# An encoder layer on one core: up- and down-projection as two phases with activations through DRAM, the up-projection with seven block products

## The chip, the core and the metric

The kernel runs on one core of one Trainium2 chip. The metric is the device time of one execution in microseconds. The kernel before took 1589.59 us, the median of three runs (1588.44 to 1590.68).

## The reference

One layer for 1536 tokens (a prompt of 512 and a sample of 1024) of width 1024: attention and a pooling mixer, an output projection into the residual, and then a feed-forward part, which the change is about.

```python
x = x + jnp.concatenate([a, p], axis=-1) @ w_out
h2 = rmsnorm(x, norm2_g)
x = x + jnp.square(jax.nn.relu(h2 @ w_up)) @ w_down    # hidden width 4096
```

All in float32. On the chip each float32 product is made of three matmuls on operands split in a high and a low part (`w_hi m_hi + w_hi m_lo + w_lo m_hi`), which the helper `three` issues.

## The kernel before

The program gives each engine its own list of instructions, in an order written out by hand; engines wait for each other by semaphores (`wait_ge`), and each engine works its list strictly from first to last. All DMAs are issued by SyncE and share one queue.

The **output projection** runs over 12 tiles of 128 tokens. TensorE makes `project_out(t)`, 48 matmuls of 512 columns, and then transposes the tile before (`transpose_x2`). VectorE adds the residual, ScalarE squares and sums (`square_x2`), GpSimd takes the power (`norm_x2`), VectorE scales (`scale_x2`), and after the transposes ScalarE copies the high part of h2 and VectorE subtracts the low part (`split_h2`). `split_c` makes the two parts of the next tile's input. h2 for all tokens stays in SBUF, high and low.

The **feed-forward part** runs over 16 chunks of 2 x 128 hidden channels (`mlp_chunk`) and in each over 3 blocks of 512 tokens. The up-projection is an ordinary product (`up_block`, 8 slices of the input width, `three` for each, 512 tokens wide). The down-projection uses the Strassen-Winograd scheme: the 2 x 2 block product (hidden channels by tokens and output columns) takes seven block products (`down_product`) instead of eight, of sums of blocks. `sum_hid` makes the sums of the hidden activations on VectorE, `sum_wd` those of the weights on GpSimd. Each product has its two PSUM banks, and VectorE adds it into one or more quarters of `yacc` in SBUF (`accumulate`). The two projections are interleaved: after each of the first products follow two slices of the next block's up-projection, after each later one three.

The names that matter: `three` lines 562 to 566, `project_out` 746 to 766, `transpose_x2` 769 to 775, ScalarE's and VectorE's parts of the feed-forward part from lines 1100 and 1434, `accumulate` line 1471, `sum_wd` lines 1712 to 1728, SyncE's loads lines 495 to 552. ScalarE's copies are all recorded at line 848, VectorE's low parts at line 1190.

## Time and profile before

| | |
|---|---|
| median of the runs | 1589.59 us |
| the profiled execution's own time | 1589.55 us |
| its span | 1587.7 us |
| TensorE busy | 1551.5 us, 98% |
| VectorE busy | 1079.1 us, 68% |
| ScalarE busy | 637.6 us, 40% |
| GpSimd busy | 386.9 us, 24% |
| mean granted TensorE clock | 0.996 |
| DMA, mean over the span | 52 GB/s |

The profile shows one execution. Busy shares tell how full an engine is, not whether it sets the end; the chain of waits, followed back from the last instruction, tells that. The records of two matmuls in a row overlap, so the time that one costs is the distance between two starts, not its record.

### The profile page before, as it was taken

The numbers are of one execution on the slowest core, as the hardware profiler recorded it, in microseconds if no ns is written. First come the engines' busy times: TensorE is split into PE (matmuls) and PEld (weight loads), VectorE is DVE, ScalarE is ACT, GpSimd is POOL, SyncE is SP. The second block draws the span as 40 slices with busy tenths as digits, with TensorE's granted clock in tenths as the row PEclk, the third lists the DMA queues.
The fourth block names the chain that finished last, engine by engine and source line by source line (L and its number), as shares of the span: only waits on it lengthen the run. The fifth ranks groups of instructions, "written<-read, shape, count | busy, mean of one in ns | idle before, by whom it ended". The sixth has DMA issues, their size and how long they took to land.

```text
span 1587.7 us, 21963 instructions
## 1 busy us (share of the span) xinstructions
PE 1551.5 (98%) x7616; PEld 1296.3 (82%) x7616; DVE 1079.1 (68%) x1285; ACT 637.6 (40%) x1016; POOL 386.9 (24%) x369
## 2 busy tenths in 40 slices
PE   6999989999999999999999999999999999999998
PEld 5999867888778888888888888888888888888886
DVE  6534479999964446767667667667667667677676
ACT  5223269999962223323323323333233233233231
POOL 3423677888850001101101101001001001011010
PEclk9999999999999999999999999999999999999999
DMA  6110021000122225011011011001101100110103
GB/s 226 47 44 17 17 81 34 12 13 13 51 99 94 81 91 225 27 41 40 26 40 40 26 40 34 32 26 40 40 26 40 40 26 26 43 37 26 40 27 146
DMA packets 28230, 82.19 MB, mean 52 GB/s; under 512 B 3105, under 2 KB 5281, under 8 KB 28193
## 3 DMA queue, kind: packets, MB, share of 16 engines
q1 hardware_dynamic: 28192, 81.70, 15.1%
q8 instruction: 22, 0.36, 0.1%
q14 instruction: 16, 0.12, 0.0%
HBM read 64.39 MB, written 12.58 MB: 48 GB/s over the span
## 4 chain that ended last, share of the span: by engine, by line
PE 70%; DVE 1%; issue 0%; DVEq 0%
PE ps L564 21%; PE ps L566 20%; PE ps L565 20%; PE ps L760 6%; PE ps L766 3%; PE ps L775 1%; DVE yacc L1471 0%; DVE hidlo L1190 0%; DVE hraw L1453 0%; DVEq L1450 0%
## 5 line engine op out<-in xcount | busy, mean ns | idle before, releaser
L1471 DVE TENSOR_TENSOR yacc<-yacc,ps 128x1024 f32<-128x1024 f32 x336 | 410.1, 1221 | 274.4 <-PE ps L566 273.1
L564 PE MATMUL ps<-h2hi,wuhi 128*128 128x512 f32 x768 | 298.9, 389 | 0.0
L566 PE MATMUL ps<-h2hi,wulo 128*128 128x512 f32 x768 | 298.8, 389 | 0.0
L565 PE MATMUL ps<-h2lo,wuhi 128*128 128x512 f32 x768 | 298.8, 389 | 0.0
L564 PE MATMUL ps<-wdhi,hidhi 128*128 128x512 f32 x672 | 262.0, 390 | 2.2 <-DVE hidlo L1190 1.7
L566 PE MATMUL ps<-wdhi,hidlo 128*128 128x512 f32 x672 | 261.5, 389 | 0.0
L565 PE MATMUL ps<-wdlo,hidhi 128*128 128x512 f32 x672 | 261.4, 389 | 0.0
L1717 POOL TENSOR_TENSOR wdraw<-wdraw,wdraw 128x512 f32<-128x512 f32 x16 | 20.8, 1298 | 738.9 <-DMA wdraw<-in_w_down 738.9
L1106 ACT ACTIVATE hraw<-ps 128x512 f32<-128x512 f32 x96 | 57.2, 596 | 314.6 <-PE ps L566 314.6
L848 ACT ACTIVATE hidhi<-hraw 128x768 fp32r<-128x768 f32 x96 | 91.4, 952 | 215.4 <-PE ps L566 215.1
L566 PEld LDWEIGHTS ps<-h2hi,wulo 128*128 128x128 f32 x768 | 144.1, 188 | 30.0
L565 PEld LDWEIGHTS ps<-h2lo,wuhi 128*128 128x128 f32 x768 | 144.2, 188 | 29.9
L564 PEld LDWEIGHTS ps<-h2hi,wuhi 128*128 128x128 f32 x768 | 144.1, 188 | 29.8
L564 PEld LDWEIGHTS ps<-wdhi,hidhi 128*128 128x128 f32 x672 | 126.1, 188 | 30.2 <-DVE hidlo L1190 2.2
L566 PEld LDWEIGHTS ps<-wdhi,hidlo 128*128 128x128 f32 x672 | 126.1, 188 | 26.3
L565 PEld LDWEIGHTS ps<-wdlo,hidhi 128*128 128x128 f32 x672 | 126.1, 188 | 26.1
L1190 DVE TENSOR_TENSOR pTlo<-ps,pThi 128x512 fp32r<-128x512 f32 x160 | 107.7, 687 | 22.8 <-ACT pThi L848 21.3
L1190 DVE TENSOR_TENSOR hidlo<-hraw,hidhi 128x768 fp32r<-128x768 f32 x96 | 110.3, 1149 | 5.8 <-ACT hidhi L848 5.8
L662 PEld LDWEIGHTS ps<-ident,prob 128*128 128x128 f32 x640 | 78.9, 141 | 33.0 <-issue 6.3
L1628 POOL TENSOR_SCALAR prob<-prob,rinv 128x1024 f32<-128x1024 f32 (+1 forms) x96 | 95.5, 1003 | 39.5 <-DVE rinv L1252 38.3
L662 PE MATMUL ps<-ident,prob 128*128 128x128 f32 x640 | 97.6, 275 | 7.0 <-POOL prob L1628 5.6
L848 ACT ACTIVATE pThi<-ps 128x512 fp32r<-128x512 f32 x160 | 95.4, 601 | 18.8 <-PE ps L662 13.9
(124 smaller groups left out, 2549.8 us busy)
## 6 DMA issues: line engine op xcount, KB each, us to landing
wuraw<-in_w_up SPq DMA_DIRECT2D x32, 512.0 KB, 3.3
wdraw<-in_w_down SPq DMA_DIRECT2D x32, 512.0 KB, 3.3
xin<-in_x SPq DMA_DIRECT2D x12, 512.0 KB, 3.4
x2in<-in_x SPq DMA_DIRECT2D x12, 512.0 KB, 3.5
out_y<-x2in SPq DMA_DIRECT2D x12, 512.0 KB, 2.9
yacc<-out_y SPq DMA_DIRECT2D x3, 2048.0 KB, 13.7
out_y<-yacc SPq DMA_DIRECT2D x12, 512.0 KB, 2.8
woraw<-in_w_out SPq DMA_DIRECT2D x2, 2048.0 KB, 7.5
```

The source lines that it names most:

```text
L564: pe.matmul(out, w_hi, m_hi, start=start, stop=False, skip_group_check=resumed)
L565: pe.matmul(out, w_hi, m_lo, start=False, stop=False, skip_group_check=resumed)
L566: return pe.matmul(out, w_lo, m_hi, start=False, stop=stop, skip_group_check=resumed)
L662: mm = pe.transpose(ps[:, 4 + k % 3, qt * P:(qt + 1) * P], prob[s.parity(pair, idx)][:, u, c0:c0 + P], ident[:])
L760: pe.matmul(ps[:, 2 * i + h], c[:, i, k], wohi[:, k, h * 512:(h + 1) * 512], start=(k == 0 and c is chi), stop=False)
L766: mm = pe.matmul(ps[:, 2 * i + h], chi[:, i, k], wolo[:, k, h * 512:(h + 1) * 512], start=False, stop=(k == KT - 1))
L848: return act.activation(out, in_, ACT.Copy, **kw)
L1106: act.activation(out, ps[:, 6 + f].rearrange("p (a c) -> p a c", a=2), ACT.Relu).then_inc(relu_done, 1)
L1190: return dve.tensor_tensor(out, a, b.bitcast(F32), ALU.subtract)
L1471: dve.tensor_tensor(q, q, gather_banks(b, o), ALU.add).then_inc(acc_done, 1)
L1628: ins = pool.tensor_scalar(p, p, rinv[:, b, q:q + 1], 1.0, ALU.mult, ALU.mult)
L1717: pool.tensor_tensor(b12, b22, b12, ALU.subtract).then_inc(wd_sum, 1)
```

## The change

The feed-forward part becomes two phases. In the **up phase** 32 steps make the hidden activations, each for one chunk of 256 hidden channels and one of two groups of 768 tokens, in which the tokens stand as two halves of 3 x 128 = 384. The product is a 2 x 2 scheme too (channels and input width, and tokens), with seven products of four slices, 384 columns each. The sums of h2 blocks are made once, while the output projection runs (`lo_h2`); for group 0 the 14 arrays (11.0 MB) go to a DRAM tensor `h2d` and come back before step 2, those of group 1 stay. The sums of w_up are made on VectorE (`sum_wu`), the products are gathered in PSUM with copies and sums (`save_u` on ScalarE, `sum_u` on VectorE), then come relu and square, then the block sums of the hidden activations (`sum_hid`), and seven blocks (1.4 MB) of each step go to DRAM (`store_hid`) from buffers `hout` that exist once.

In the **down phase** 8 chunks of 512 hidden channels by 3 units of 512 tokens take 7 products each; a product now runs over two hidden slices in PSUM, 12 matmuls, before it is accumulated, so there are 168 accumulations and not 336. The hidden blocks are loaded in three parts per unit (`load_hid`), split by `hi_part` and `lo_part`, and the weights of the next chunk are split meanwhile (`hi_wd`, `lo_wd`) into the other of two sets of buffers.

The core of the diff, SyncE first (its order of stores and loads):

```diff
+            def load_wu(w, c):
+                if not (isinstance(w, int) and w == 0):
+                    sp.wait_ge(wu_lo, SLOTS * w)
+                sp.dma_start(wuraw[:], w_up[bass.ds(2 * c, 2)].rearrange("f p k n -> p f k n")).then_inc(wu_in, 16)
...
+            for p in range(TT):
+                if p == TT - 1:
+                    sp.wait_ge(c_hi, TT)
+                    sp.wait_ge(c_lo, TT)
+                    load_wu(0, 0)
+                store_x2(p)
+                if p in (3, 5, 7):
+                    store_h2((p - 3) // 2)
+                if p + 2 < TT:
+                    load_x2(p + 2)
+            def store_hid(n, c, g):
+                for i, (ready, count) in enumerate(((raw_done, 4 * n + 3), (hid_sum, 4 * n + 3), (hid_sum, 4 * n + 4))):
+                    sp.wait_ge(ready, count)
+                    sp.dma_start(hd[i][bass.ds(c, 1), :, 3 * (1 - g):3 * (1 - g) + 3].rearrange("a p q s c -> (a p) q s c"),
+                                 hout[i][:]).then_inc(h_out[i], 16)
+            load_wu(1, 1)
+            sp.wait_ge(out_done, TT)
+            sp.wait_ge(xT2_done, TT)
+            for o in range(SLOTS):
+                for q in range(QT_TILES):
+                    sp.wait_ge(h2_stored[q], 16 if q == 1 else 32)
+                sp.dma_start(h2[0][o][:].rearrange("p a q k c -> p a (q k c)").bitcast(F32),
+                             h2d[2 * o:2 * o + 2].rearrange("a p q c -> p a (q c)")).then_inc(h2_in[o], 16)
...
+            store_hid(0, 0, 1)
+            load_wu(2, 2)
+            store_hid(1, 1, 1)
```

TensorE, with what each product waits for:

```diff
+            def up_product(s, w, g, par, o):
+                pe.wait_ge(wu_lo, SLOTS * w + o + 1)
+                if isinstance(s, int) and s == 0:
+                    pe.wait_ge(h2_lo, SLOTS * 5 + 2 if o < 2 else SLOTS * 6)
+                if isinstance(s, int) and s == 2:
+                    pe.wait_ge(h2_in[o], 16)
+                if not (isinstance(s, int) and s < 2):
+                    if o == 0:
+                        pe.wait_ge(relu_done, 4 * s - 4)
+                    if o == 1:
+                        pe.wait_ge(u_sum, 3 * s - 5)
+                    if o == 3:
+                        pe.wait_ge(u_sum, 3 * s - 3)
                 if o == 2:
+                    pe.wait_ge(u_copied, 3 * s + 1)
+                if o == 4:
+                    pe.wait_ge(u_copied, 3 * s + 2)
+                if o == 5:
+                    pe.wait_ge(u_copied, 3 * s + 3)
+                if o == 6:
+                    pe.wait_ge(u_sum, 3 * s + 2)
+                for k in range(4):
+                    mm = three(up_bank(par, o), wuhi[o][:, k], wulo[o][:, k], h2[g][o][:, 0, :, k], h2[g][o][:, 1, :, k],
+                               o in OPENS and k == 0, k == 3, o not in OPENS)
+                mm.then_inc(up_done, 1)
+            def up_step(s, w, g, par):
+                for o in range(SLOTS):
+                    up_product(s, w, g, par, o)
...
+            def down_product(n, z, u, o):
+                m = UNITS * n + u
+                if u == 0:
+                    pe.wait_ge(wd_lo, SLOTS * n + o + 1)
+                if o in (0, 2, 5):
+                    pe.wait_ge(hid_lo, 3 * m + part_of(o)[0] + 1)
+                if isinstance(m, int) and m == 0 and o in (1, 3):
+                    pe.wait_ge(relu_done, 8 * CHUNKS)
+                    pe.wait_ge(u_sum, 6 * CHUNKS)
                 pe.wait_ge(acc_done, SLOTS * m + (2, 6, SLOTS + 1, SLOTS, SLOTS + 3, SLOTS + 4, SLOTS + 5)[o])
-                banks = gather_banks(b, o)
-                for j in range(2):
...
+                banks = down_banks(u, o)
+                i, j = part_of(o)
+                for q in range(2):
+                    for k in range(2):
+                        mm = three(banks[:, q], hidhi[i][:, k, q, j], hidlo[i][:, k, q, j],
+                                   wdhi[z][o][:, k], wdlo[z][o][:, k], o in OPENS and k == 0, k == 1, o not in OPENS)
                 mm.then_inc(down_done, 1)
...
+            for p in range(1, TT):
+                project_out(p)
+                transpose_x2(p - 1)
+            up_product(0, 0, 1, 0, 0)
+            up_product(0, 0, 1, 0, 1)
             transpose_x2(TT - 1)
```

ScalarE, relu and square of a step, and its order in the down phase:

```diff
+            def square_relu(s, par, k):
+                if k < 3:
+                    act.wait_ge(u_sum, 3 * s + k + 1)
+                    src = (u1, u1, u2)[k][:].rearrange("p (q c) -> p q c", q=QT_TILES)
+                else:
+                    act.wait_ge(up_done, SLOTS * s + SLOTS)
+                    src = up_bank(par, 6)
+                out = h12[:] if k == 3 else out_slot((0, 5, 1)[k])
+                if not (isinstance(s, int) and s == 0):
+                    act.wait_ge(hid_sum, 4 * s)
+                    if k < 3:
+                        act.wait_ge(h_out[(0, 2, 0)[k]], 16 * s)
+                act.activation(out, src, ACT.Relu).then_inc(relu_done, 1)
+                act.wait_ge(relu_done, 4 * s + k + 1)
+                act.activation(out, out, ACT.Square).then_inc(raw_done, 1)
...
+            def down_chunk(n, z, last=False):
+                for u in range(UNITS):
+                    m = UNITS * n + u
+                    for i in range(3):
+                        if not (last and u == UNITS - 1):
+                            hi_part(m + 1, i)
+                        if not last:
+                            for o in (((), (0, 1), ()), ((2,), (3,), ()), ((4,), (5,), (6,)))[u][i]:
+                                hi_wd(n + 1, 1 - z, o)
             act.wait_ge(z_act, GROUPS)
```

VectorE, the last tiles of the output projection, the sums of an odd tile of h2, the order of a step, and that of a chunk of the down phase:

```diff
+            for p in range(1, TT):
+                if p + 1 < TT:
+                    split_c(p + 1)
+                else:
+                    for o in range(2):
+                        lo_wu(0, o)
+                    for k in range(4):
+                        sum_wu(0, k)
+                    for o in range(2, SLOTS - 1):
+                        lo_wu(0, o)
+                residual(p)
+                if p % 2 == 0:
+                    scale_x2(p)
+                    lo_h2(p - 1)
+                else:
+                    lo_h2(p - 1)
+                    scale_x2(p)
+            lo_h2(TT - 1)
+            lo_wu(0, SLOTS - 1)
...
+                raw = {o: h2_full(q, o) for o in (2, 3, 4, 5)}
+                dve.wait_ge(xT2_done, p + 1)
+                dve.wait_ge(h2_b11, q + 1)
+                dve.tensor_tensor(raw[4], h2_bank(q, 2), raw[5], ALU.subtract).then_inc(h2_sum, 1)
+                dve.wait_ge(h2_hi, SLOTS * q + 3)
+                dve.wait_ge(h2_sum, 4 * q + 1)
+                dve.tensor_tensor(raw[2], h2_bank(q, 3), raw[4], ALU.subtract).then_inc(h2_sum, 1)
+                dve.wait_ge(h2_sum, 4 * q + 2)
+                dve.tensor_tensor(raw[3], raw[2], raw[5], ALU.subtract).then_inc(h2_sum, 1)
+                dve.wait_ge(h2_sum, 4 * q + 3)
+                dve.tensor_tensor(raw[5], h2_bank(q, 1), raw[2], ALU.subtract).then_inc(h2_sum, 1)
+                minus(h2_half(q, 6, 1), h2_bank(q, 3), h2_half(q, 6, 0)).then_inc(h2_lo, 1)
+                dve.wait_ge(h2_sum, 4 * q + 4)
+                for n, o in enumerate((4, 2, 3, 5)):
+                    dve.wait_ge(h2_hi, SLOTS * q + 4 + n)
+                    minus(h2_half(q, o, 1), raw[o], h2_half(q, o, 0)).then_inc(h2_lo, 1)
...
+            def up_step(s, par, prep=None, late=None, sums=True, first_down=False):
+                if sums:
+                    for k in range(4):
+                        sum_hid(s - 1, k)
+                if late is not None:
+                    lo_wu(late, 6)
+                if first_down:
+                    lo_wd(0, 0, 0)
+                if prep is not None:
+                    lo_wu(prep, 0)
+                sum_u(s, par, 0)
+                if prep is not None:
+                    lo_wu(prep, 1)
+                if first_down:
+                    lo_wd(0, 0, 1)
+                    lo_wd(0, 0, 2)
+                    lo_part(0, 0)
+                sum_u(s, par, 1)
+                if prep is not None:
+                    sum_wu(prep, 0)
+                    sum_wu(prep, 1)
+                if first_down:
+                    lo_wd(0, 0, 3)
+                sum_u(s, par, 2)
+                if prep is not None:
+                    sum_wu(prep, 2)
+                    sum_wu(prep, 3)
+                    for o in range(2, 6):
+                        lo_wu(prep, o)
+                if first_down:
+                    for o in range(4, SLOTS):
+                        lo_wd(0, 0, o)
+            def lo_wd(n, z, o):
+                dve.wait_ge(wd_hi, SLOTS * n + o + 1)
                 if o == 2:
-                    dve.wait_ge(wd_sum, 4 * c + 4)
...
+            def down_chunk(n, z, last=False):
+                for u in range(UNITS):
+                    m = UNITS * n + u
+                    more = not (last and u == UNITS - 1)
+                    def lo_wds(*slots):
+                        for o in slots:
+                            if not last:
+                                lo_wd(n + 1, 1 - z, o)
+                    accumulate(n, u, 0)
+                    accumulate(n, u, 1)
+                    if more:
+                        lo_part(m + 1, 0)
+                    accumulate(n, u, 2)
+                    lo_wds(*((), (2,), (4,))[u])
+                    accumulate(n, u, 3)
+                    lo_wds(*((0,), (), ())[u])
+                    accumulate(n, u, 4)
+                    if more:
+                        lo_part(m + 1, 1)
+                    accumulate(n, u, 5)
+                    lo_wds(*((1,), (3,), (5,))[u])
+                    accumulate(n, u, 6)
+                    if more:
+                        lo_part(m + 1, 2)
+                    lo_wds(*((), (), (6,))[u])
+            up_step(0, 0, prep=1, sums=False)
...
+            up_step(2 * CHUNKS - 1, 1, late=CHUNKS, first_down=True)
+            lo_part(0, 1)
+            for k in range(4):
+                sum_hid(2 * CHUNKS - 1, k)
+            lo_part(0, 2)
+            down_chunk(0, 0)
```

## Rows read from the trace of the kernel before

**Rows 1.** The page, busy time by engine: busy us, share, instructions.
```profile
PE 1551.5 (98%) x7616; PEld 1296.3 (82%) x7616; DVE 1079.1 (68%) x1285; ACT 637.6 (40%) x1016; POOL 386.9 (24%) x369
```

**Rows 2.** The page, chain that ended last: by engine, by line.
```profile
PE 70%; DVE 1%; issue 0%; DVEq 0%
PE ps L564 21%; PE ps L566 20%; PE ps L565 20%; PE ps L760 6%; PE ps L766 3%; PE ps L775 1%; DVE yacc L1471 0%; DVE hidlo L1190 0%; DVE hraw L1453 0%; DVEq L1450 0%
```

**Rows 3.** Busy time by stretch, its length first, then engines, clock, DMA.
```profile
599.50:1567.50 968.00, 968.00 (x4277) 801.57 (x4276) 676.77 (x756) 304.45 (x432) 82.98 (x66) 1.00 0.13 43
```

**Rows 4.** Timeline, TensorE at its end: start us, us, instruction.
```profile
1582.78 0.40 PE L566 MATMUL ps<-wdhi,hidlo 128*128 128x512 f32 x1
```

**Rows 5.** The chain in order of time, output projection: start us, us.
```profile
457.46 8.77 PE ps L760 x32
469.86 7.25 PE ps L760 x32
583.20 3.63 PE ps L766 x16
598.64 0.87 PE ps L775 x8
```

**Rows 6.** Timeline of 256-column matmuls (first, last of 44); group of their loads.
```profile
74.20 0.28 PE L565 MATMUL ps<-hTlo,wihi 128*128 128x256 f32 x1
...
79.35 0.28 PE L566 MATMUL ps<-hThi,wilo 128*128 128x256 f32 x1
...
L565 PEld LDWEIGHTS ps<-hTlo,wihi 128*128 128x128 f32 x192 | 37.3, 194 | 0.2
```

**Rows 7.** Groups of instructions (busy us, mean ns); one stretch of three sums.
```profile
L1471 DVE TENSOR_TENSOR yacc<-yacc,ps 128x1024 f32<-128x1024 f32 x336 | 410.1, 1221 | 274.4 <-PE ps L566 273.1 <-issue 0.9
L1190 DVE TENSOR_TENSOR wdlo<-wdraw,wdhi 128x512 fp32r<-128x512 f32 x96 | 65.5, 684 | 0.0
L1453 DVE TENSOR_TENSOR hraw<-hraw 128x256 f32<-128x256 f32 x192 | 82.7, 431 | 6.1 <-ACT hraw L1108 1.9
L848 ACT ACTIVATE hidhi<-hraw 128x1024 fp32r<-128x1024 f32 x48 | 50.7, 1056 | 80.1 <-PE ps L566 79.9 <-DVE hraw L1453 0.2
L1728 POOL TENSOR_TENSOR wdraw<-wdraw,wd_t 128x512 f32<-128x512 f32 x16 | 20.8, 1302 | 0.0
1568.59 1.48 DVE L1453 TENSOR_TENSOR hraw<-hraw 128x256 f32<-128x256 f32 x3
```

**Rows 8.** Timeline of the steps after one tile's output projection.
```profile
492.71 1.22 DVE L1387 TENSOR_TENSOR x2in<-x2in,ps 128x1024 f32<-128x1024 f32 x1 [4.74 <-PE ps L766]
493.97 1.06 ACT L1066 ACTIVATE junk<-x2in 128x1024 f32<-128x1024 f32 x1 [8.75 <-DVE x2in L1387]
495.47 0.55 POOL L1538 TENSOR_TENSOR rsx<-msx,mexp 128x1 f32<-128x1 f32 x1
```

**Rows 9.** DMA: one stretch at full rate; issues, KB each, us to landing.
```profile
612.00:616.00 4.00, 4.00 (x20) 3.30 (x19) 3.12 (x5) 3.72 (x6) 1.43 (x2) 1.00 1.03 417
wuraw<-in_w_up SPq DMA_DIRECT2D x32, 512.0 KB, 3.3
rope<-in_rope SPq DMA_DIRECT2D x12, 64.0 KB, 1.9
pscale<-in_pool_scale SPq DMA_DIRECT2D x1, 2.0 KB, 8.8
```

**Rows 10.** TensorE after being idle, and the clock granted (before DMA share).
```profile
203.73 0.47 PE L644 MATMUL ps<-KA,Qs 128*128 128x512 f32 x1 [2.22 <-ACT prob L920]
205.00:208.00 3.00, 3.00 (x16) 2.90 (x16) 2.96 (x4) 1.38 (x4) 2.47 (x3) 0.57 0.00 0
456.25 0.50 PE L564 MATMUL ps<-dhi,wphi 128*128 128x512 f32 x1 [1.25 <-POOL dlo L1666]
1572.13 0.49 PE L564 MATMUL ps<-wdhi,hidhi 128*128 128x512 f32 x1 [1.73 <-DVE hidlo L1190]
```

More of the change, by code:

```diff
@@ L157, in hybrid_layer @@
+        hin = [at(f"hin{i}", hin_at[i], [2, 2, len(PARTS[i]), P]) for i in range(3)]
         ps = ctx.enter_context(nc.psum_tensor("ps", [P, 8, 512], F32))
@@ new lines, in load_ahead @@
+            def load_ahead(n, u, last=False):
+                if u == 0 and not last:
+                    load_wd(n + 1)
+                m = n, u + 2
+                if u:
+                    m = n + 1, u - 1
+                if not (last and u):
+                    for i in range(3):
+                        load_hid(*m, i)
+            with sp.Fori(0, DOWNS // 2 - 1) as h:
+                for z in range(2):
+                    for u in range(UNITS):
+                        load_ahead(h * 2 + z, u)
@@ new lines, in _ @@
+            up_step(0, 0, prep=1)
+            up_step(1, 1, late=1)
+            up_step(2, 0, prep=2)
+            with act.Fori(2, CHUNKS) as c:
+                up_step(2 * c - 1, 1, late=c)
+                up_step(2 * c, 0, prep=c + 1)
+            up_step(2 * CHUNKS - 1, 1, late=CHUNKS, first_down=True)
+            hi_part(0, 1)
+            hi_part(0, 2)
+            down_chunk(0, 0)
+            down_chunk(1, 1)
+            with act.Fori(1, DOWNS // 2 - 1) as h:
+                for z in range(2):
+                    down_chunk(h * 2 + z, z)
@@ L1736, in rope_tables @@
+            sum_wd(0, 0)
+            sum_wd(1, 1)
+            with pool.Fori(1, DOWNS // 2) as h:
+                for z in range(2):
+                    sum_wd(h * 2 + z, z)
 def rope_tables():
```

821 lines of the change are left out of this document (443 added, 378 removed).

## The prediction

> **What bounds the kernel now.** I read the page's busy row first: TensorE is busy 98% of the span, VectorE 68% [rows 1]. The chain of waits puts 70% of the span on TensorE and 61% on the three matmul lines of the helper `three`, in equal parts [rows 2]. The busy times by stretch then say where: from 599.5 to 1567.5 us, the feed-forward part, TensorE is never idle, in 4277 matmuls [rows 3]. Eight of these are transposes that take 0.87 us together [rows 5], so a matmul of 512 columns takes (968.0 - 0.87)/4269 = 0.2266 us. The last matmul starts at 1582.78 [rows 4]. All of the feed-forward part is 4320 such matmuls: 979 us, and with the transposes 979.8. It lasts 599.51 to 1583.0, so 3.7 us are lost, in the last unit. There is no slack on TensorE to win, so only fewer columns help, and every wait that the new order puts on TensorE costs its full length.
>
> The profiled execution took 1589.55 us for a span of 1587.7; the 1.85 us around it stay. It equals the median of the runs (1589.59).
>
> **Removed: one product in eight of the up-projection.** Before: 96 blocks (32 slices of the hidden width, 3 token blocks) of 8 x 3 matmuls of 512 columns, 2304. After: 32 steps of 7 products of 4 x 3 matmuls of 384 columns, 2688. No row has 384 columns. 256 columns take (79.35 - 74.20)/43 = 0.1198 us [rows 6]; the middle of that and 0.2266 is 0.1732. Ends: the rate per column of the 512 form gives 0.1700, that of the 256 form 0.1797. I take the middle, since both widths lie about 13 ns over columns/2.4 GHz. 2304 x 0.2266 - 2688 x 0.1732 = 522.1 - 465.6 = **-56.5 us** (ends -65.1 and -39.1). The new moving operand is read as three pieces of 128 columns; no row shows that, and I take it as free, as the ends hold a few per cent of it. The down-projection has 8 x 3 x 7 x 12 = 2016 matmuls, as before.
>
> The Trainium skill (TensorE: Matmul & The Clock Gate, "Back-to-back issue gap") gives N/2.4 + 2.5 ns for an isolated gap, 162.5 ns at 384 columns. By that the up-projection would take 436.8 us and be 29 us shorter still. But its value for 512 is 215.8, where this trace has 226.6, so I don't take it for the sum.
>
> **Removed: the 3.7 us at the end.** It came from a last unit that no up-projection covered. In the last unit now a product takes 12 x 0.2266 = 2.72 us and an accumulation 1.22 [rows 7], so nothing waits: **-3.7**. The 205 us of VectorE that half the accumulations save were beside TensorE: 0.
>
> **Added: work on h2 while the output projection runs.** A tile there takes 7.3 + 3.6 + 0.87 = 11.8 us of TensorE [rows 5]. VectorE's operations on 512 columns take 0.684, 0.61 apart, or 0.79 apart if each waits for the one before (at 256 columns one takes 0.43 and dependent ones stand 0.53 apart [rows 7]). For an odd tile it now has four dependent sums and five low parts, 6.1 us. They start when residual, ScalarE's square, GpSimd's power and the scaling are through, 4.7 us after the projection's end (residual to power, 492.71 to 495.47 + 0.55 [rows 8], then 1.2), and end at 10.8; the next transposes are due at 11.8. Hidden with 1.0 us to spare, the next `split_c` with 0.6: 0, at most 1 us on each of 5 tiles.
>
> **A. First up product.** Before, TensorE went straight on at 599.5. Now it needs tile 10's h2. At 597.6 VectorE is done with tile 9 (586.8 + 10.8), and then comes the new first weight chunk, ahead of `residual(11)`: 2 low parts, 4 dependent sums, 4 low parts, 1.2 + 3.2 + 2.4 = 6.8 us. So residual at 604.4, square to 606.8, two copies, two low parts: 608.8. **+9.3**.
>
> **B. The third product** needs all of tile 11: its transposes end at 613.9, then four sums, low part, four low parts, 6.3 us: 620.2. **+6.3**.
>
> **C, D. Behind the h2 reload.** SyncE issues the load of weight chunk 1 only when chunk 0's last low part is done (620.8), and it lands 4.7 later (3.3 for half its size, and half a megabyte more at full rate [rows 9]); ScalarE stands at it and TensorE's fifth product waits until 628.8: **+4.4**. Behind it in the same queue go 7 loads, 11.0 MB. At 410 GB/s [rows 9] the 12.1 MB end at 622.0 + 29.4 = 651.4. Only then comes `store_hid(0)`, for which `square_relu` of step 1 waits (`h_out`, the output buffer is single). One store more (1 us) and its completion (1.5) make 653.9; square_relu and `save_u(1)` follow, 1.5 us. The fifth product of step 1 starts at 655.5 and not at 643.4: **+12.1**. That transfers of one queue land in order is read from 2 KB that took 8.8 us behind others where 64 KB took 1.9 [rows 9]. Were they served side by side, D would be 0, and at 340 GB/s 18 us.
>
> **The 30 steps after that** take 12 x 7 x 0.1732 = 14.55 us each. I add 7.3 us on VectorE and 8 on ScalarE a step; the tightest place is `save_u(1)` of the odd steps, queued behind the weight sums and four low parts of the step before: it ends about 0.8 to 1.1 us before it is due. 0; it would be up to 1 us in 15 steps.
>
> **E. Up to down.** In step 31 VectorE's `lo_wd(0,0,2)` waits for GpSimd's third and fourth sum of 1024 columns (1.3 us for 512 [rows 7]; I take 2.2, with 2.6 as the end); `sum_u(1)` is queued behind it and the last up product waits for that: about 4 us. After the last product, square_relu, hi_part, lo_part, four sums and lo_part stand before `accumulate(0,0,0)`, for which the third down product waits. That is 9.4 us in all, **+9.4** (4 to 12).
>
> **F. One wait in each chunk of the down phase.** At the first unit of a chunk ScalarE runs `hi_part(m+1,1)` when product 4 ends, then `hi_wd(0)`; VectorE has `lo_wd(0)` queued before `accumulate 4`; product 6 waits for that accumulation. From the start of product 5: 0.16 + 0.1 (end of product 4 and hop), hi_part on 1536 columns 1.4, hi_wd 1.05, lo_wd 1.15, accumulation 1.22, hop 0.1 = 5.2 against 2.72 of cover. 2.5 us in 7 chunks: **+17.5** (0 to 21).
>
> **The clock.** After an idle of 1.25 us at 456.25 the granted clock fell to 1.2 GHz, and the 32 matmuls that take 7.25 took 8.77 [rows 5, 10]; after 2.22 us at 203.73 too (0.57 granted in 205 to 208); after 1.73 at 1572 not [rows 10]. So 1.5 us a fall: A, D and E surely (B and C's is inside D), F at about half: 6.5 x 1.5, **+9** (0 to 15).
>
> Sum: -56.5 - 3.7 + 9.3 + 6.3 + 4.4 + 12.1 + 9.4 + 17.5 + 9 = +7.8. Span 1595.5, time **1597**. That is slower by 0.5%.
>
> **Rivals.**
> 1. The wait of F is not there: VectorE isn't held by `lo_wd(0)`, since ScalarE's two copies come early enough. For it: VectorE has only 15 of 19 us a unit, and a chain under 2.72 us costs nothing. Against it: four rows in series already make 4.8. Then -17.5 and -5 of clock: 1575, faster. It decides at 2.72 us from product 4's end. Chance 0.27.
> 2. Columns cost less than I think: the 13 ns over columns/2.4 go away at 384 (2688 x 0.1600 = 430), -35 us: 1562, faster. Against it: two widths show the 13 ns. This is about what the skill's formula named above gives (its 162.5 ns, -29). Chance 0.04.
> 3. Weight loads bind: a load's record is 191 to 194 ns [rows 6], longer than a matmul of 384 columns now takes. If each had to end before the next began, 2688 x 0.191 = 513, +48: 1645. Against it: at 256 columns the same loads stand beside a pace of 120. Chance 0.03.
> 4. The steady steps are tighter than drawn (1 us in 15 steps, 1 in 5 tiles, 2 in E and D): +24: 1618. For it: margins under 1.1 us in three places. Chance 0.12.
> 5. The waits are a little shorter each, and the sum comes out level: 1589. Chance 0.1.
> My forecast: 0.44.
>
> **How the numbers follow.** A measurement of this kernel tells a change from none at about 0.2%, 3.2 us. Faster: rivals 1 and 2, 0.31. Same: rival 5 and a little of the forecast, 0.12. Slower: the rest of the forecast, rivals 3 and 4, 0.57. The range goes from rival 1 with 6 us below it, 1569, to rival 4, 1618; what is left out is rivals 2 and 3 and the tails. The likeliest case alone spans 1588 to 1610.
>
> **What would show it.** The 384-column matmuls start 0.173 us apart. TensorE is idle for some 9 us just after 599.5, 6 us before the third up product, then 4, then 12 where it is ScalarE's copy of u that releases it and ScalarE waits for a DMA of the output blocks. In the down phase TensorE is idle seven times for 2.5 us, released by an accumulation; between the steps of the up phase it is idle nowhere. I am wrong if the idle TensorE time after 599.5 is under 40 us in all, or if the pace is outside 0.170 to 0.180.

## The result and the profile after

The changed kernel took 1625.46 us (median of 4, 1617.37 to 1627.6), the kernel before 1589.13: a ratio of 1.0218, 95% interval [1.0182, 1.0254]. It is slower, as forecast, but by 36 us and not by 8, and above the range of the prediction (1569 to 1618). The profiled execution took 1625.35 us for a span of 1623.6, at a mean granted clock of 0.976.

The page after, busy time by engine (answers to [rows 1]) and the chain that ended last ([rows 2]):

```profile
PE 1520.8 (94%) x8000; PEld 1346.7 (83%) x8000; DVE 1041.2 (64%) x1290; ACT 731.3 (45%) x1231; POOL 386.7 (24%) x337
...
PE 77%; DVE 6%; issue 5%; POOL 5%; ACT 4%; DMA 3%; SPq 0%; DVEq 0%; ACTq 0%; POOLq 0%
```

TensorE is busy 31 us less and its share falls from 98 to 94%: it now waits. Where, the busy times by stretch say (columns as in [rows 3]; the clock, third from the end, is the granted share of 2.4 GHz, and the last two lines are single stretches at the lower level, 0.50 or 1.2 GHz, "half clock" below):

```profile
600.50:675.00 74.50, 44.45 (x223) 43.66 (x224) 30.16 (x49) 26.14 (x50) 0.74 (x2) 0.82 0.55 220
675.00:1090.00 415.00, 415.00 (x2397) 415.00 (x2396) 204.28 (x355) 212.34 (x412) 2.51 (x2) 1.00 0.36 135
1133.00:1618.00 485.00, 457.62 (x1943) 374.20 (x1942) 365.31 (x280) 127.22 (x116) 73.87 (x28) 0.96 0.37 120
605.50:612.00 6.50, 2.60 (x8) 2.63 (x9) 3.25 (x4) 2.71 (x5) 0.74 (x2) 0.50 0.20 81
1138.50:1144.50 6.00, 5.59 (x13) 4.51 (x14) 5.26 (x5) 0.09 (x1) 1.97 (x2) 0.50 0.30 85
```

The middle of the up phase is full: 2397 matmuls of 384 columns in 415 us, 0.1731 us each, at clock 1.00. The loss is in the first three steps (30 of 74.5 us idle, clock 0.82) and in the down phase (27 us idle, clock 0.96). Every wait of TensorE over 1 us after 600.5, from its timeline (start us, us, instruction, idle before and releaser; what was [rows 10] before), in the order of the prediction's terms, A, B, C, D, then E (four), then F (seven):

```profile
609.40 0.66 PE L729 MATMUL ps<-h,wuhi 128*128 128x384 f32 x1 [9.08 <-DVE h L1432]
622.08 0.66 PE L729 MATMUL ps<-h,wuhi 128*128 128x384 f32 x1 [6.08 <-DVE h L1432]
630.97 0.41 PE L729 MATMUL ps<-h,wuhi 128*128 128x384 f32 x1 [2.73 <-ACT u L1028]
658.13 0.66 PE L729 MATMUL ps<-h,wuhi 128*128 128x384 f32 x1 [12.33 <-ACT u L1028]
1095.37 0.41 PE L729 MATMUL ps<-h,wuhi 128*128 128x384 f32 x1 [1.92 <-ACT u L1028]
1101.64 0.41 PE L729 MATMUL ps<-h,wuhi 128*128 128x384 f32 x1 [1.87 <-ACT u L1028]
1109.99 0.41 PE L729 MATMUL ps<-h,wuhi 128*128 128x384 f32 x1 [3.95 <-DVE u L1735]
1122.44 0.47 PE L729 MATMUL ps<-wdhi,hidhi 128*128 128x512 f32 x1 [3.10 <-DVE yacc L1802]
1138.91 0.77 PE L729 MATMUL ps<-wdhi,hidhi 128*128 128x512 f32 x1 [5.31 <-DVE yacc L1802]
1202.08 0.50 PE L729 MATMUL ps<-wdhi,hidhi 128*128 128x512 f32 x1 [3.05 <-DVE yacc L1802]
1264.66 0.80 PE L729 MATMUL ps<-wdhi,hidhi 128*128 128x512 f32 x1 [3.56 <-DVE yacc L1802]
1325.78 0.80 PE L729 MATMUL ps<-wdhi,hidhi 128*128 128x512 f32 x1 [2.20 <-DVE yacc L1802]
1389.10 0.79 PE L729 MATMUL ps<-wdhi,hidhi 128*128 128x512 f32 x1 [4.33 <-DVE yacc L1802]
1453.64 0.80 PE L729 MATMUL ps<-wdhi,hidhi 128*128 128x512 f32 x1 [4.32 <-DVE yacc L1802]
1518.08 0.80 PE L729 MATMUL ps<-wdhi,hidhi 128*128 128x512 f32 x1 [4.20 <-DVE yacc L1802]
```

What D waits for shows on ScalarE, whose copy of `u` releases it: before that ScalarE waits for a store of the output blocks.

```profile
656.53 0.52 ACT L1311 ACTIVATE hout<-u 128x384 f32<-128x384 f32 x1 [16.04 <-DMA hd<-hout]
```

The starts of all matmuls give the account, term by term. For each one, the gap to the next start less the pace of its width is waiting, or clock where the granted clock is half and the gap only doubled. TensorE's part from the last transposes of the output projection to its end lasts 1018.8 us after (600.15 to 1618.99; before 599.51 to 1583.0, 983.5): 2688 x 0.1733 + 2016 x 0.2266 + 0.9 of transposes = 923.5, and 95.3 of losses.

| us lost in | predicted | measured |
|---|---|---|
| A, B, C, D, waiting | 32.1 | 30.9 |
| E, waiting | 9.4 | 11.5 |
| F, waiting | 17.5 | 28.8 |
| clock, all | 9 | 22.2 (5.7 beside A to D, 1.6 at E, 14.9 at F) |
| rest | 0 | 1.9 |

The waits here are up to 0.3 us longer each than in the rows, as a first matmul after a wait has a longer record. The down phase alone, F and its clock, lost 43.7 us.

What the seven waits of F are made of shows in three engines' timelines just before one of them (start us, us, instruction; at 1389.10 TensorE goes on):

```profile
1381.89 2.41 POOL L2044 TENSOR_TENSOR wdraw<-wdraw 128x1024 f32<-128x1024 f32 x1 [45.36 <-DMA wdraw<-in_w_down]
1384.48 2.35 POOL L2053 TENSOR_TENSOR wd_t<-wdraw 128x1024 f32<-128x1024 f32 x1 [0.18 <-POOL wdraw L2044]
...
1382.08 1.49 ACT L1028 ACTIVATE hidhi<-hin 128x1536 fp32r<-128x1536 f32 x1 [7.02 <-PE ps L731]
1383.48 1.98 ACT L1028 ACTIVATE wdhi<-wdraw 128x1024 fp32r<-128x1024 f32 x2
...
1384.55 3.36 DVE L1432 TENSOR_TENSOR wdlo<-wdraw,wdhi 128x1024 fp32r<-128x1024 f32 x1 [3.97 <-ACT wdhi L1028]
1387.83 1.21 DVE L1802 TENSOR_TENSOR yacc<-yacc,ps 128x1024 f32<-128x1024 f32 x1
```

The order is the one the prediction drew: `hi_part`, `hi_wd(0)`, `lo_wd(0)`, accumulate 4, product 6. But `lo_wd(0)` (the "split" of slot 0: VectorE subtracts the high part of a weight block from it) takes 3.36 us, where the prediction had 1.15. It is recorded from 1384.55, GpSimd's second sum from 1384.48 to 1386.83, and the split ends 1.08 us behind that sum, as if it had stood still until GpSimd was through. One chunk earlier the split began first, and there it is GpSimd that takes longer:

```profile
1323.36 1.23 DVE L1432 TENSOR_TENSOR wdlo<-wdraw,wdhi 128x1024 fp32r<-128x1024 f32 x1 [3.96 <-ACT wdhi L1028]
1323.42 3.39 POOL L2053 TENSOR_TENSOR wd_t<-wdraw 128x1024 f32<-128x1024 f32 x1 [0.18 <-POOL wdraw L2044]
```

The wait follows the split. In chunks 1 to 6 the splits of slot 0 take 2.07, 2.40, 1.23, 3.36, 3.34 and 3.23 us and the waits are 3.05, 3.56, 2.20, 4.33, 4.32 and 4.20: each time 0.97 to 1.16 us more than the split.

### The profile page after: what moved, and what is told of

Its sections match the earlier page's. It is cut to its first block, busy times and chain, and to the rows that moved or that the text cites. A ratio compares the mean times of both kernels' runs of the same rounds, so it can differ in the third digit from the quotient of the medians.

```text
span 1623.6 us, 23483 instructions
## 1 busy us (share of the span) xinstructions
PE 1520.8 (94%) x8000; PEld 1346.7 (83%) x8000; DVE 1041.2 (64%) x1290; ACT 731.3 (45%) x1231; POOL 386.7 (24%) x337
## 2 busy tenths in 40 slices
DMA packets 68789, 193.55 MB, mean 119 GB/s; under 512 B 5504, under 2 KB 7680, under 8 KB 68736
## 4 chain that ended last, share of the span: by engine, by line
PE 77%; DVE 6%; issue 5%; POOL 5%; ACT 4%; DMA 3%; SPq 0%; DVEq 0%; ACTq 0%; POOLq 0%
PE ps L729 20%; PE ps L730 20%; PE ps L731 20%; PE ps L925 5%; PE ps L827 3%; PE ps L931 2%; DMA wdraw<-in_w_down 1%; POOL prob L1954 1%; PE ps L842 1%; PE ps L843 1%; PE ps L809 1%; DMA hd<-hout 1%; PE ps L811 1%; DVE yacc L1802 1%; DVE nmax L1487 1%
## 5 line engine op out<-in xcount | busy, mean ns | idle before, releaser
L729 PE MATMUL ps<-h,wuhi 128*128 128x384 f32 x896 | 303.0, 338 | 38.0 <-ACT u L1028 18.9
L730 PE MATMUL ps<-h,wuhi 128*128 128x384 f32 x896 | 302.1, 337 | 0.0
L731 PE MATMUL ps<-h,wulo 128*128 128x384 f32 x896 | 301.9, 337 | 0.0
L1802 DVE TENSOR_TENSOR yacc<-yacc,ps 128x1024 f32<-128x1024 f32 x168 | 204.5, 1218 | 92.2 <-PE ps L731 91.8
L1028 ACT ACTIVATE hidhi<-hin 128x1024 fp32r<-128x1024 f32 (+1 forms) x72 | 86.6, 1205 | 352.5 <-PE ps L731 347.5
L2044 POOL TENSOR_TENSOR wdraw<-wdraw 128x1024 f32<-128x1024 f32 x8 | 19.1, 2391 | 790.2 <-DMA wdraw<-in_w_down 790.2
L729 PEld LDWEIGHTS ps<-h,wuhi 128*128 128x128 f32 x896 | 170.3, 190 | 39.8 <-issue 34.6
L1735 DVE TENSOR_TENSOR u<-u,ps 128x384 f32<-128x384 f32 x96 | 53.1, 553 | 198.9 <-PE ps L731 198.6
L730 PEld LDWEIGHTS ps<-h,wuhi 128*128 128x128 f32 x896 | 170.5, 190 | 0.0
L731 PEld LDWEIGHTS ps<-h,wulo 128*128 128x128 f32 x896 | 170.3, 190 | 0.0
L1432 DVE TENSOR_TENSOR hidlo<-hin,hidhi 128x1024 fp32r<-128x1024 f32 (+1 forms) x72 | 115.3, 1601 | 6.6 <-ACT hidhi L1028 6.6
L1311 ACT ACTIVATE hout<-u 128x384 f32<-128x384 f32 x96 | 50.4, 525 | 147.6 <-DVE u L1735 128.0
```

The costliest lines, as they stand in the source:

```text
L729: pe.matmul(out, w_hi, m_hi, start=start, stop=False, skip_group_check=resumed)
L730: pe.matmul(out, w_hi, m_lo, start=False, stop=False, skip_group_check=resumed)
L731: return pe.matmul(out, w_lo, m_hi, start=False, stop=stop, skip_group_check=resumed)
L1028: return act.activation(out, in_, ACT.Copy, **kw)
L1311: act.activation(out, src, ACT.Relu).then_inc(relu_done, 1)
L1432: return dve.tensor_tensor(out, a, b.bitcast(F32), ALU.subtract)
```

## The experiments

The theory after the traces: all the loss is waits by order in the engines' queues, at four places, and the down phase costs more than predicted as VectorE's splits stand still beside GpSimd's sums and as each wait brings half clock. The rival: the new traffic (193.55 MB in place of 82.19) or the engines themselves set the time, so that a wait removed comes back elsewhere. Each ratio is to the kernel before, run beside it on the same chip; the kernel after stands at 1.0218.

**Split 0 of the next weight chunk behind accumulate 5.**

```diff
-                    lo_wds(*((0,), (), ())[u])
                     accumulate(n, u, 4)
...
-                    lo_wds(*((1,), (3,), (5,))[u])
+                    lo_wds(*((0,), (3,), (5,))[u])
...
-                    lo_wds(*((), (), (6,))[u])
+                    lo_wds(*((1,), (), (6,))[u])
```

> VectorE's low part of the next chunk's weights no longer stands ahead of accumulation 4: slot 0 is moved behind accumulation 5, slot 1 behind the last low part of the unit. Nothing is left out. Theory (the waits of TensorE in the down phase come from that order, and each brings a stretch at 1.2 GHz): the seven waits, 27.0 us in the changed kernel, go below 5 us, the time at half clock in the down phase (14.9 us of loss) below 5 us, and the time falls by 30 to 38 us, to about 1590. Rival (VectorE and GpSimd are too full in the first unit of a chunk, so the wait only moves to the next unit): waits of 2 us or more appear at the third product of the second unit, and the gain is under 15 us.

Measured: 1594.65 us (1591.64 to 1596.54), ratio 1.0034 [1.0019, 1.0048], 31 us under the changed kernel. The seven waits at product 6 are gone; what stays are seven of 0.7 to 1.8 us at the third product of the second unit, 9 us together where under 5 were expected. The clock in the down phase:

```profile
1133.00:1585.00 452.00, 443.02 (x1947) 364.69 (x1946) 353.56 (x279) 127.14 (x116) 82.76 (x28) 1.00 0.40 129
```

So one VectorE operation a chunk in the wrong gap costs 31 us; by the account above it is 18.7 of waiting (28.8 to 10.1) and 14.9 of clock (to 0), between the two profiled executions.

**TensorE kept busy through the wait of F**, by 14 matmuls that write to a free bank.

```diff
+                        if o == 6 and u == 0 and not last:
+                            for _ in range(14):
+                                pe.matmul(ps[:, 7], hidhi[2][:, 0, 0, 0], wdhi[z][5][:, 0], start=True, stop=True)
                         down_product(n, z, u, o)
```

> In the first unit of each down chunk TensorE makes 14 matmuls of 512 columns into an unused bank ahead of product 6 (3.2 us at full clock), so it isn't idle while it waits; the order is otherwise that of the changed kernel. Theory (the low clock follows from TensorE being idle in these waits): nearly no half clock in the down phase after its first chunk, the waits keep their end (set by VectorE), and the time falls by 8 to 15 us although TensorE does 22 us more work. Rival (the clock falls for another reason, for instance the DMA traffic of this phase): half clock stays, and the time is the same or up to 22 us longer.

Measured: 1616.07 us (1615.16 to 1617.92), ratio 1.0170 [1.0153, 1.0187]: 9 us less with more work on the engine. The granted clock from 1133 to 1608 us is 1.00. From the end of product 5 to product 6 the seven places take 25.3 us in place of 28.1; in four of them the fill itself (3.17 us) now sets it. So the waits are filled rather than removed, and what the run gives back is for the most part clock: 14.9 us in the down phase, of which 3 are lost again at E (4.7 us of clock there in place of 1.6).

**GpSimd's sums later**: the first waits until the first unit of the chunk in work is through.

```diff
                 pool.wait_ge(wd_in, 16 * n + 16)
+                if not (isinstance(n, int) and n == 0):
+                    pool.wait_ge(down_done, SLOTS * (UNITS * n - UNITS + 2))
```

> GpSimd begins the weight sums of the next chunk only when product 6 of the first unit is done, so it is idle while VectorE makes the low part that product 6 waits for. Theory (in the changed kernel VectorE's two-operand SBUF operations take 2.1 to 3.4 us instead of 1.22 where GpSimd works at the same time): low part 0 takes 1.22 in each chunk, and the wait of chunks 1 to 6 becomes 2.5 to 2.7 us each, 16 us together, where it was 21.7; the time falls by 5 to 9 us. Rival (the length of these waits has to do with something else, such as the clock): they keep their 2.2 to 4.3 us and the time stays.

Measured: 1613.16 us (1612.37 to 1616.11), ratio 1.0154 [1.0137, 1.0171]. The waits at product 6 fall to 2.19 to 2.72 us (five of the seven are 2.19 or 2.20), and one of 0.45 to 1.08 appears in the unit behind each. The splits of slot 0 all take 1.22 or 1.23 us now. No half clock was left from 1133 us on, which I had not expected: 12 us are gained in place of 5 to 9.

**The store of step 0 behind four of the seven h2 reloads.**

```diff
-            for o in range(SLOTS):
...
+            for o in range(4):
+                load_h2(o)
...
             store_hid(0, 0, 1)
+            for o in range(4, SLOTS):
+                load_h2(o)
             load_wu(2, 2)
```

> SyncE issues the store of step 0's output blocks after four of the seven reloads of h2 instead of behind all. Theory (one queue, served in order): the 12.3 us wait of TensorE in step 1 becomes 1 to 3 us, the half clock after it is mostly gone, and the time falls by 11 to 14 us; the last h2 array lands before step 2 needs it. Rival (transfers of one queue share the engines, and the 12 us come from the volume of 11 MB): the wait stays above 8 us, or moves to step 2.

Measured: 1612.99 us (1611.6 to 1617.38), ratio 1.0155 [1.0138, 1.0172]. D's wait is gone, and a third of it is back one step later, since weight chunk 2 now comes behind the last reloads:

```profile
648.04 0.41 PE L734 MATMUL ps<-h,wuhi 128*128 128x384 f32 x1 [0.80 <-ACT u L1033]
667.35 0.66 PE L734 MATMUL ps<-h,wuhi 128*128 128x384 f32 x1 [4.50 <-ACT u L1033]
```

**The order before the first up product** (ScalarE's part and the product's wait; VectorE likewise takes `residual(11)` and `lo_h2(10)` before three of the sums).

```diff
-                    for o in range(SLOTS - 1):
+                    hi_wu(0, 0)
+                    hi_wu(0, 1)
+                    hi_h2(p - 1)
+                    square_x2(p)
+                    for o in range(2, SLOTS - 1):
                         hi_wu(0, o)
+                    continue
...
-                    pe.wait_ge(h2_lo, SLOTS * 5 + 2 if o < 2 else SLOTS * 6)
+                    pe.wait_ge(h2_lo, SLOTS * 5 + (2, 2, 5, 6, 7, 7, 7)[o])
```

> Order of the last output-projection iteration changed: ScalarE splits the h2 half of tile 10 before it squares tile 11, VectorE takes the residual add of tile 11 and the two h2 splits behind the first two weight splits and leaves three weight sums and the weight splits 2 to 5 for behind them; the products of step 0 wait for their own h2 block product instead of for all seven. Theory (the wait A, 9.1 us, is only VectorE's and ScalarE's order: the eight weight operations that stand ahead of the residual add): the wait of the first up product falls from 9.1 to 2 to 4 us, the transposes of tile 11 start some 6 us earlier, the wait of the third product (B, 6.1) falls by 1 at most, since its chain of ten VectorE operations stays: 1625 falls to 1615 to 1618. Rival (the wait is the data's: the last output products themselves end too late): no change. D stays, 12 us, as its transfers begin 8 us earlier but last as long, or grows by what the steps before it have shrunk.

Measured: 1616.41 us (1615.1 to 1618.84), ratio 1.0169 [1.0152, 1.0186]. A falls from 9.08 to 2.33 us, B only to 5.58; C grows from 2.73 to 3.58. A was order; B is a chain of VectorE operations on the last tile.

**The order in the last up step** (VectorE's part; ScalarE saves product 0 first, and GpSimd's sums for down-weight chunk 0 start with step 31).

```diff
-                if first_down:
-                    lo_wd(0, 0, 0)
...
                 if first_down:
+                    lo_wd(0, 0, 0)
                     lo_wd(0, 0, 1)
-                    lo_wd(0, 0, 2)
-                    lo_part(0, 0)
                 sum_u(s, par, 1)
...
                     accumulate(n, u, 0)
+                    if first and u == 0:
+                        for k in range(4):
+                            sum_hid(2 * CHUNKS - 1, k)
```

> Order of the last up step changed: ScalarE saves the first product ahead of the first down-weight split, VectorE adds the second and fifth product ahead of the weight splits that wait for GpSimd, GpSimd starts the sums of down-weight chunk 0 one step later (behind VectorE's weight sums), and VectorE takes the first accumulate of the down phase ahead of the sums of the last step. Theory (E, four waits of 10.8 us and 1.6 us of half clock, is the order in the last step): they fall to 1 to 3 us in all: 1625 falls to 1614 to 1617. Rival (E is the transfers': the weight chunk and the first parts of the hidden layer come late): the waits move to the first or second down product with their size, no gain over 3 us.

Measured: 1619.8 us (1617.01 to 1624.82), ratio 1.0200 [1.0183, 1.0218]: under the changed kernel's median, but the ranges overlap. In the profile E's four waits of 10.8 us became two of 7.6, and the first wait of F grew from 5.31 to 8.15. This one failed: 1614 to 1617 was expected. GpSimd's sums now stand beside VectorE's last weight splits, which take 0.69 us each alone, and `sum_u(0)` is queued behind these. The first of two that take 2.9:

```profile
1089.89 2.89 DVE L1431 TENSOR_TENSOR wulo<-wuraw,wuhi 128x512 fp32r<-128x512 f32 x1
```

The 8.15 us are something else: ScalarE waits for the load of down-weight chunk 1, as it already did before the first wait of F in the changed kernel (1.83 us there).

```profile
1135.92 2.00 ACT L1028 ACTIVATE wdhi<-wdraw 128x1024 fp32r<-128x1024 f32 x2 [4.67 <-DMA wdraw<-in_w_down]
```

**All seven splits spread**, one to a gap between accumulates (the first unit behind accumulate 5; the second behind 0, 3 and 5; the third behind 0, 2 and 5). ScalarE's halves change order with them.

```diff
                     accumulate(n, u, 0)
+                    lo_wds(*((), (1,), (4,))[u])
...
                     accumulate(n, u, 2)
-                    lo_wds(*((), (2,), (4,))[u])
+                    lo_wds(*((), (), (5,))[u])
                     accumulate(n, u, 3)
-                    lo_wds(*((0,), (), ())[u])
+                    lo_wds(*((), (2,), ())[u])
...
-                    lo_wds(*((1,), (3,), (5,))[u])
+                    lo_wds(*((0,), (3,), (6,))[u])
```

> F alone, further than in the run with the first two splits moved: VectorE's seven splits of the next down-weight chunk lie one in each gap of the accumulates (first unit behind accumulate 5; second unit behind 0, 3 and 5; third unit behind 0, 2 and 5), ScalarE's halves go before them. Theory (a product waits for an accumulate that stands behind a split; each gap between accumulates is 1.5 us and holds one split of 1.22): the 10 us of waits that were left at the third product of the second unit fall to 0 to 3, no half clock in the down phase: 1594.7 falls to 1584 to 1589. Rival (the 10 us are the memory's or GpSimd's slowing of VectorE wherever the splits lie): they come back at another product, 1592 to 1596.

Measured: 1584.94 us (1582.85 to 1588.0), ratio 0.9972 [0.9960, 0.9983]. With this alone the kernel is faster than before. In its down phase TensorE is idle for 0.6 us in 445:

```profile
1133.00:1578.00 445.00, 444.39 (x1956) 366.32 (x1954) 359.39 (x280) 128.55 (x117) 79.06 (x28) 1.00 0.40 132
```

GpSimd's sums still take up to 3.91 us here, and three splits meet them and take 2.30; in this order hardly anybody waits for it.

**All four places at once** (SyncE's part; in steps 0 and 2 the splits of the next weight chunk also go behind the saves).

```diff
-            load_wu(1, 1)
...
+            load_h2(0)
+            load_h2(1)
+            load_wu(1, 1)
+            load_h2(2)
...
             store_hid(0, 0, 1)
             load_wu(2, 2)
+            for o in range(3, 6):
+                load_h2(o)
             store_hid(1, 1, 1)
+            load_h2(6)
```

> All four waits at once: the orders of the two runs on the first product and on the step from up to down, the spread splits of the down phase, and for C and D: the first two h2 reloads go ahead of the load of weight chunk 1, the third behind it, then the store of step 0, the load of weight chunk 2, three reloads, the store of step 1 and the last reload; in steps 0 and 2 the splits of the next weight chunk come behind the saves and the fifth product's sum. Theory (every wait is an order in a queue, none the data's or the engine's): A and B 15 to 7, C 4.4 to 0, D 12.3 to 0 to 4 (11 MB of reloads, two weight chunks and two stores have to move in some 46 us of steps 0 to 3, which is just what the queues give), E 12.4 to 3, F and its clock 42 to 3: 1625 falls to 1552 to 1568, under the kernel before (1589.6) by 1.4 to 2.4%. Rival (contention of the memory queues in steps 0 to 3 and of GpSimd with VectorE in the down phase gives the waits back in other places): 1575 to 1600.

Measured: 1567.61 us (1566.9 to 1572.35), ratio 0.9871 [0.9854, 0.9888]. In steps 0 to 3 TensorE still waits, with D at 4.33 us; and between up and down with four of 4.31, 3.03, 1.00 and 3.54 us, where I had expected 3 in all. The four single runs (first product 9.0, up to down 5.7, spread 40.5, store early 12.5) gain 67.7 us when added, together they gain 57.9. So most of it adds up, and at most 10 us are the rival's, given back elsewhere; the runs of the changed kernel themselves lie 10 us apart.

**The same with what its trace left** (the cuts are against the run before this one): one reload more ahead of the store of step 0, two of step 0's weight splits behind the sums of the last tile, GpSimd's first sum behind the last step's first `sum_u`, and the work of the first down unit laid between its accumulates.

```diff
             load_h2(2)
+            load_h2(3)
...
             store_hid(0, 0, 1)
...
-                    pool.wait_ge(up_done, SLOTS * (2 * CHUNKS - 1))
+                    pool.wait_ge(u_sum, 3 * (2 * CHUNKS - 1) + 1)
...
+                    if start:
+                        lo_part(0, 1)
+                        lo_wd(0, 0, 4)
                     accumulate(n, u, 1)
```

> The kernel with all four waits mended, with what its trace left: one more h2 reload ahead of the store of step 0; two of step 0's weight splits behind the h2 chain of the last tile; GpSimd's first sum for down-weight chunk 0 only behind the first sum of the last step; in the first unit of the down phase the weight splits 4 to 6, the parts and the sums of the last step lie one by one between the accumulates, the last step's sums first. Theory (the 4.3 us wait of step 2 is the last reloads that the store of step 0 held up; the 4.3 us wait of the last up step is VectorE's two weight splits of 2.9 us beside GpSimd's sums, and each brought a stretch of half clock of some 2.5 us): both waits fall under 1.5 us without half clock, the third product's wait (B) falls from 5.6 to 4.4, the wait of 3.0 at the start of the down phase to 1: 1567.6 falls to 1552 to 1560. Rival (the memory queues give what they can in steps 0 to 3): the step 2 wait stays at 3 to 5, 1560 to 1565.

Measured: 1560.64 us (1559.36 to 1561.09), ratio 0.9820 [0.9806, 0.9833]: 1.8% faster than the kernel before, 4% than the one after. Its page, and all the waits of TensorE of 1 us or more:

```profile
PE 1501.4 (96%) x8000; PEld 1334.3 (86%) x8000; DVE 1033.6 (66%) x1290; ACT 730.9 (47%) x1231; POOL 393.1 (25%) x337
```

```profile
602.45 0.41 PE L737 MATMUL ps<-h,wuhi 128*128 128x384 f32 x1 [2.33 <-DVE h L1447]
612.60 0.66 PE L737 MATMUL ps<-h,wuhi 128*128 128x384 f32 x1 [4.87 <-DVE h L1447]
630.58 0.41 PE L737 MATMUL ps<-h,wuhi 128*128 128x384 f32 x1 [1.77 <-ACT u L1036]
655.25 0.41 PE L737 MATMUL ps<-h,wuhi 128*128 128x384 f32 x1 [1.54 <-issue]
1086.69 0.76 PE L737 MATMUL ps<-wdhi,hidhi 128*128 128x512 f32 x1 [3.98 <-ACT h L1319]
1092.26 0.47 PE L737 MATMUL ps<-wdhi,hidhi 128*128 128x512 f32 x1 [1.00 <-issue]
1117.58 0.77 PE L737 MATMUL ps<-wdhi,hidhi 128*128 128x512 f32 x1 [6.01 <-DVE yacc L1823]
```

Half of the expectation failed: D fell as expected (4.33 to 1.54) and B most of the way (to 4.87), but the two waits from up to down only changed their place (now 3.98 and 6.01). Before the second ScalarE waits for the late load of down-weight chunk 1:

```profile
1109.57 2.01 ACT L1036 ACTIVATE wdhi<-wdraw 128x1024 fp32r<-128x1024 f32 x2 [7.35 <-DMA wdraw<-in_w_down]
```

Hence 1560.6, just above the expected 1552 to 1560. It lies in the rival's range, but not for the rival's reason, as the wait of step 2 did go.

**Three of GpSimd's four sums narrowed** from chunk 1 on, to 32 of 512 columns. This kernel leaves out most of three sums, so its output is not the layer's; it is run for its time alone. The second sum keeps its full width.

```diff
-                pool.tensor_tensor(b12, b22, b12, ALU.subtract).then_inc(wd_sum, 1)
+                pool.tensor_tensor(b12[:, :, 0:w], b22[:, :, 0:w], b12[:, :, 0:w], ALU.subtract).then_inc(wd_sum, 1)
```

> The kernel after, with three of GpSimd's four sums per down-weight chunk (from chunk 1 on) on 32 of 512 columns, so that part of the sums is left out; everything else and all waits as they were. Theory (F, 27 us of waits and 13 us of clock in place of the 17.5 predicted, is GpSimd's sums slowing VectorE's splits from 1.22 to 2 to 3.4 us; without them the wait is ScalarE's queue of part 1 and split 0, 2.2 us, which brings no half clock): product 6 waits 2.0 to 2.4 us in chunks 1 to 6, no half clock there: 1625 falls to 1606 to 1613. Rival (the splits are slow by themselves, or by ScalarE or the transfers): 1620 to 1627, waits of 3 to 5 us as before.

Measured: 1617.97 us (1615.83 to 1618.89), ratio 1.0176 [1.0160, 1.0191]; between the two. The waits of chunks 1 to 6 fall to 2.34 to 2.69 us, with one of 3.49 (the six together 21.7 before, 16.2 now); the first grows to 6.99. So taking the three away is worth 5.5 us of waits in these six chunks. It isn't the whole of the standstill: the second sum still lies beside the split of slot 0, which takes 1.37 to 2.51 us in them. In the chunk whose wait is 2.52:

```profile
1387.21 1.55 DVE L1432 TENSOR_TENSOR wdlo<-wdraw,wdhi 128x1024 fp32r<-128x1024 f32 x1 [3.97 <-ACT wdhi L1028]
1385.27 2.40 POOL L2054 TENSOR_TENSOR wd_t<-wdraw 128x1024 f32<-128x1024 f32 x1 [0.18 <-POOL wdraw L2045]
```

With GpSimd later, where no sum lay beside it, the same six waits came to 13.4, 8.2 less. But here the half clock stayed (13 us in the down phase), which this theory had tied to the longer waits.

## Why the prediction was wrong

The places and the order of the waits were right. Two terms failed: F's wait was sized without VectorE standing still beside GpSimd (17.5 us forecast, 28.8 measured), and the clock was given too few falls and too low a price (9 forecast, 22.2 measured).

- **One product in eight** (-56.5): right. 0.1731 us a matmul in the full stretch against the 0.1732 taken, and no cost of the three-piece operand shows. The Trainium skill's formula (TensorE: Matmul & The Clock Gate, "Back-to-back issue gap") would have had 162.5 ns. The trace has 173.1, and the second rival, which needed about 160, is refuted.
- **The 3.7 us at the end** and **the work on h2** (0): right. The last unit runs without a wait; TensorE's idle time between 452 and 600 us is 2.3 us against 1.5 before.
- **A** (9.3): 9.08. **B** (6.3): 6.08. **C** (4.4): 2.73. **D** (12.1): 12.33. That D is the order of one queue, the run with the store early shows: the same bytes, the store earlier, and the wait is 0.80 (with 4.50 one step later, for the load that now comes last).
- **The 30 steady steps** (0): right, no wait from 675 to 1090 us. The third rival is refuted, and so is the fourth in its largest part; of its rest, E came out 1.4 us longer.
- **E** (9.4): 10.8, in the four places named or next to them. GpSimd's sum takes 2.39 us, where I took 2.2.
- **F** (17.5): the first failed step. "`lo_wd` 1.15" was scaled up from the 0.684 of a group of 512-column splits [rows 7] that hardly differ among each other. In the changed kernel a split takes 1.22 us where GpSimd rests, and 2.07 to 3.36 us in the six places where it began beside a sum already running. Six of the seven waits are longer than the 2.5 predicted, the first (5.31) also because down-weight chunk 1 lands late: 27.0 us in the rows. With the sums out of the way they are 2.2 to 2.7 (the run with GpSimd later), so the chain itself had been drawn about right. The Trainium skill says it outright (SBUF — State Buffer, "SBUF: two separate sides"): VectorE with two SBUF inputs and GpSimd take turns for whole instructions at a shared port pair. This trace agrees: the split ends 1.08 us behind GpSimd's sum, and accumulates, which read one operand from PSUM, stay at 1.21 us in between. The trace of before could have told: its low parts of the hidden activations, 128x1024, take 1.22 us alone and 1.38 to 1.76 in the 15 cases beside one of GpSimd's weight sums, but I took durations from the groups' means. One of the 15, and the sum beside it:

```profile
1208.19 1.76 DVE L1190 TENSOR_TENSOR hidlo<-hraw,hidhi 128x1024 fp32r<-128x1024 f32 x1
1207.58 1.29 POOL L1717 TENSOR_TENSOR wdraw<-wdraw,wdraw 128x512 f32<-128x512 f32 x1 [49.50 <-DMA wdraw<-in_w_down]
```

- **The clock** (9): the second failed step, and the larger: 22.2. Two things were off. I counted 6.5 falls, and there were 11: each of the seven waits of F brought one where I had half of them, and B had one of its own where I had counted it with D's. And each cost 2 us and not 1.5 (6.5 x 1.5 is also 9.75 and not 9). That the clock is worth about this, the filled wait shows: with 22 us of work added the time falls by 9.4, and no half clock is left there.

The two together are 24.5 of the 27.3 us by which the losses after 600 us exceed the sum, E 2.1 and the rest 1.9, less 1.2 that A to D came out under. The first rival ("VectorE isn't held by `lo_wd(0)`") was wrong for this kernel, but it was an order that could be had: where the split is moved, the time falls to 1594.7 and, spread, to 1584.9. Its price, 22.5 us with the clock, was too low by the same two terms; the spread is worth 40.5.

## What to carry to other kernels

Where TensorE is full, the columns removed were worth what their pace said (56 us here), and what decided the change was whether an operation that nobody needed yet stood in front of one that TensorE waited for: here the splits in the wrong gaps cost 40 us, more than two thirds of what a product in eight had won. Lay optional work one operation to a gap between accumulates, and price an operation of VectorE by what GpSimd does beside it, not by its group's mean. A wait of 2 to 4 us that recurs has to be priced with the clock that follows it, half as much again in this down phase. Where a phase needs a large reload, put the stores that free a single buffer ahead of the part that is not yet needed.

## What the runs showed that I had not expected

- VectorE's operations with two inputs in SBUF and GpSimd's sums lengthen each other, whichever comes second: GpSimd's sum of 128x1024 is 2.39 us alone and up to 3.40 beside a split of 1.22, the split up to 3.36.
- The length of a wait doesn't settle whether half clock follows. Waits of 2.19 or 2.20 us at product 6 were followed by none in the run with GpSimd later (five of them), and all three by one in the run with the first product's order. Nor does the order of the down phase settle it: in the run from up to down, four waits at product 6 are 2.20 us long, and half clock follows the first of them and not the other three. Two such waits from the timelines, the run with the first product's order first, and behind each the stretch after it (columns as above, the clock is third from the end):

```profile
1449.91 0.50 PE L729 MATMUL ps<-wdhi,hidhi 128*128 128x512 f32 x1 [2.20 <-DVE yacc L1812]
```

```profile
1451.00:1454.50 3.50, 3.50 (x10) 2.76 (x9) 3.50 (x3) 0.06 (x1) 0.00 (x0) 0.51 0.17 24
```

```profile
1445.22 0.50 PE L729 MATMUL ps<-wdhi,hidhi 128*128 128x512 f32 x1 [2.20 <-DVE yacc L1802]
```

```profile
1445.20:1455.00 9.80, 9.78 (x42) 7.83 (x43) 9.63 (x8) 2.23 (x3) 6.31 (x3) 1.00 0.36 109
```

What decides between them stays open, and with it whether the later sums themselves took the half clock out of the run with GpSimd later, or whether it could have come out otherwise with the same waits.
